# A recurrent layer with its projections inside the head-pair loop, and with them in a phase of their own

## The reference, cut to what matters

```python
def even_layer(h, g, w_in, shift_mu, ...):
    p = rmsnorm(h, g) @ w_in                                   # (1024 x 1024) @ (1024 x 4224)
    p_shift = token_shift(p[..., :SHIFT_WIDTH], shift_mu)      # p + (p_prev - p) * mu
    p_r, p_k, p_v, p_wd, p_ad = jnp.split(p_shift, ...)        # 512, 512, 512, 64, 64 columns
    gate_a, q_b, k_b, v_b, gate_b = jnp.split(p[..., SHIFT_WIDTH:], ...)   # 512 each
    y_a = rwkv7_mix(p_r, p_k, p_v, p_wd, p_ad, ...) * jax.nn.silu(gate_a)
    y_b = chunk_attention(q_b, k_b, v_b, att_bias) * jax.nn.silu(gate_b)
    return h + jnp.concatenate([y_a, y_b], axis=-1) @ w_out

def rwkv7_mix(...):      # 8 heads of 64
    decay = exp(-exp(w(p_wd)));  a = sigmoid(a0 + p_ad @ a2)
    kk = k * k_k, divided by its norm over each head;  k = k * (1 + (a - 1) * k_a)
    state = state * decay + (state @ -kk) (kk * a)^T + v k^T   # a scan over the 1024 tokens
    y = group norm of (state @ r) * lnx_g + lnx_b + bonus(r, k, v)

def chunk_attention(...):  # 8 heads of 64, chunks of 64 tokens, each sees itself and 8 chunks to the left
```

## Time and profile before

| what | us |
|---|---|
| median of 3 runs (4167.7 to 4175.02) | 4168.65 |
| the profiled execution, its own time | 4164.67 |
| its span, first to last instruction | 4162.9 |
| TensorE busy in it | 3959.1 (95%) |
| DVE, ACT, POOL busy | 1739.9, 1324.5, 1197.7 |

### The profile page before, as it was taken

How to read it: one execution, slowest core, us unless ns; L and a number is a source line. 1 busy time by engine, 2 the same in 40 slices (tenths; PEclk the granted TensorE clock), 3 DMA queues, 4 the chain that set the end, 5 groups by cost and what they waited for, 6 DMA issues and landing times.

```text
span 4162.9 us, 59315 instructions
## 1 busy us (share of the span) xinstructions
PE 3959.1 (95%) x26210; PEld 3198.6 (77%) x26210; DVE 1739.9 (42%) x2696; ACT 1324.5 (32%) x2213; POOL 1197.7 (29%) x613
## 2 busy tenths in 40 slices
PE   8899999999999999899999889999999999999997
PEld 4757676665998897677687777897888988888877
DVE  2545454533340258762215463332187432332344
ACT  3232323232332243562212353212275312212133
POOL 1202010102114356761232102343102523332354
PEclk9999999999999999999999999999999999999999
DMA  3101010003111121010011100130100211111111
GB/s 91 32 2 32 2 32 3 17 11 108 42 41 41 51 71 51 26 31 31 28 54 42 40 1 23 49 107 28 51 1 21 72 61 51 47 45 51 51 41 41
DMA packets 164977, 168.68 MB, mean 41 GB/s; under 512 B 8176, under 2 KB 152432, under 8 KB 164720
## 3 DMA queue, kind: packets, MB, share of 16 engines
q1 hardware_dynamic: 164720, 164.89, 12.5%
HBM read 156.48 MB, written 8.39 MB: 40 GB/s over the span
## 4 chain that ended last, share of the span: by engine, by line
PE 80%; DVE 9%; ACT 5%; POOL 4%; issue 2%; DMA 0%; POOLq 0%; DVEq 0%; ACTq 0%; SPq 0%
PE pair L641 16%; PE pair L643 16%; PE pair L642 16%; PE pair L606 10%; PE pair L629 3%; PE pair L617 2%; PE pair L1137 1%; PE pair L596 1%; PE pair L1327 1%; PE pair L791 1%; POOL H L3472 1%; PE pair L1297 1%; ACT BIG L2084 1%; PE pair L783 1%; POOL W_r L3414 1%
## 5 line engine op out<-in xcount | busy, mean ns | idle before, releaser
L641 PE MATMUL pair<-XT_r,W_r 128*128 128x512 f32 x1744 | 693.8, 398 | 8.5 <-ACT BIG L2022 1.9
L642 PE MATMUL pair<-BIG_r,W_r 128*128 128x512 f32 x1624 | 632.2, 389 | 0.0
L3414 POOL TENSOR_TENSOR W_r<-W,W_r 128x2048 fp32r<-128x2048 f32 (+1 forms) x74 | 327.1, 4420 | 741.2 <-ACT W_r L1475 741.2
L643 PE MATMUL pair<-XT_r,W_r 128*128 128x512 f32 x1232 | 480.1, 390 | 0.0
L641 PE MATMUL pair<-W_r,BIG_r 128*128 128x256 f32 (+1 forms) x1280 | 417.9, 326 | 1.5 <-DVE MIX_r L2774 0.4
L606 PE MATMUL pair<-XT,W 128*128 128x512 f32 x928 | 405.5, 595 | 3.2 <-POOL MIX L3287 2.2
L641 PEld LDWEIGHTS pair<-XT_r,W_r 128*128 128x128 f32 x1744 | 327.4, 188 | 85.3 <-issue 10.6
L643 PE MATMUL pair<-W_r,BIG_r 128*128 128x256 f32 (+1 forms) x1152 | 380.3, 330 | 0.0
L642 PEld LDWEIGHTS pair<-BIG_r,W_r 128*128 128x128 f32 x1624 | 305.0, 188 | 68.9 <-issue 6.7
L606 PEld LDWEIGHTS pair<-XT,W 128*128 128x128 f32 x928 | 175.1, 191 | 220.1 <-issue 218.6
L643 PE MATMUL pair<-W_r,MIX_r 128*128 128x256 f32 x960 | 271.6, 283 | 0.0
(11 more groups left out here) (440 smaller groups left out, 7744.3 us busy)
## 6 DMA issues: line engine op xcount, KB each, us to landing
W<-w_in SPq DMA_DIRECT2D x29, 1024.0 KB, 5.5
W<-w_in_e SPq DMA_DIRECT2D x33, 512.0 KB, 6.6
MIX<-w_up SPq DMA_DIRECT2D x15, 1024.0 KB, 5.3
MIX<-w_down SPq DMA_DIRECT2D x15, 1024.0 KB, 4.9
W<-w_in_o SPq DMA_DIRECT2D x12, 1024.0 KB, 5.0
W<-w_in SPq DMA_DIRECT2D x17, 512.0 KB, 4.1
H<-x SPq DMA_DIRECT2D x16, 512.0 KB, 9.2
W<-w_out SPq DMA_DIRECT2D x7, 1024.0 KB, 5.3
```

Of the source, the lines that this page charges most:

```text
L641: E.matmul(b[:, 0:n], lh, rh, start=k == ks[0], stop=False)
L642: E.matmul(b[:, 0:n], lh, rl, start=False, stop=False)
L643: mm = E.matmul(b[:, 0:n], ll, rh, start=False, stop=k == ks[-1])
L3414: G.tensor_tensor(WLO[k % 2][:, 0:n], WSTAGE[k % 2][:, 0:n], WHI[k % 2][:, 0:n], ALU.subtract).then_inc(*s_split.mark("split", k))
```

## The change

It splits the even layer into two phases.

Phase one (`proj`): the normalised rows are kept as a high part `XH` (rounded by ACT) and a low part `XL` (DVE's subtraction). All products of the layer follow one another as split products over 17 weight pieces (`PROJ`): lora, then k, r, v of the recurrence and of the band for two pairs at a time, then both gates. ACT and DVE evict them, gates through Silu, to eight slots in `MIX`; SP writes 29 rows of 128 x 1024 to a tensor `rows` in DRAM. The shifts and the norm of pair 0 run beside.

Phase two: the four head pairs without products. SP loads raw rows, q, k, v and gates back, each behind the operation that frees its buffer. A pair is now "late" (decay, operands, transposes), the factor rounds woven with "tail" (normalising the previous pair; three of its multiplications and additions and the gate go to POOL), and the last chunk rounds woven with "early" (shifts and norm of the next pair). The norm's square root and reciprocal become Ln and Exp on ACT. The pacing is 212 to 192. The keep-up matmuls of the recurrence are removed. `pe_even` keeps only the last tail ahead of the output projection.

```diff
-        RW_ROUNDS, BAND_STEPS = 224, 224
+        RW_ROUNDS, BAND_STEPS = 212, 192
...
-        KEEP_UP.update({("rwkv", "v_tr", c, 0): 14 for c in range(4)})
...
+        PROJ = ([("lora", 0, 0, 1536)] + [(what, g, pp, base + g * HALF + pp * Q) for pp in range(2)
+                                          for what, base in (("rkv", 0), ("qkv", 2176)) for g in (1, 0, 2)] +
+                [(what, 0, pp, base + pp * Q) for what, base in (("gate_r", 1664), ("gate_b", 3712)) for pp in range(2)])
+        FIRST_PIECE = -len(PROJ)
+        SPILL = [(what, g, 2 * pp + ct) for what, g, pp, _ in PROJ[1:] for ct in range(2)
+                 if (what, pp, ct) != ("rkv", 0, 0)]
+        ROW = {b: n for n, b in enumerate(SPILL)}
...
+        def pe_proj():
+            early = pe_early(0)
+            for j, (what, g, pp, _) in enumerate(PROJ):
+                k = FIRST_PIECE + j
+                if (what, g) == ("qkv", 2):
+                    wh, wl = chunk(k)
+                    for t in range(NT):
+                        ts = slice(t * P, (t + 1) * P)
+                        pe_split(proj, every, (what, g, pp, t), Q, KD, lambda kk: (XH[:, kk, ts], XL[:, kk, ts]),
+                                 lambda kk: (wh[:, kk, :], wl[:, kk, :]), done("split", k))
+                else:
+                    width = P if what == "lora" else Q
+                    wh, wl = chunk(k, KD, width)
+                    for c0 in range(0, width, P):
+                        for half in range(2):
+                            hs = slice(half * HALF, (half + 1) * HALF)
+                            pe_split(proj, every, (what, g, 2 * pp + c0 // P, half), HALF, KD,
+                                     lambda kk: (wh[:, kk, c0:c0 + P], wl[:, kk, c0:c0 + P]),
+                                     lambda kk: (XH[:, kk, hs], XL[:, kk, hs]), done("split", k),
+                                     done("ev", "begin", "tr", 4 * half + 3, 1))
+                proj.pe.note("chunk_free", k)
+                if j > 3:
+                    next(early, None)
+            run(early)
...
+        def pe_early(c):
+            ring = for_rw if c else every
+            yield from nothing(3)
+            for hf in range(2):
+                b = ring.open("rwkv", "norm", c, hf)
+                pe.wait_ge(*ring.free("rwkv", "norm", c, hf))
+                pe.wait_ge(*done("rwkv", "kk_sq", c))
+                E.matmul(b[:, :], head_ones[:, :], BT[:, hf * HALF:(hf + 1) * HALF], start=True,
+                         stop=True).then_inc(*rw.pe.mark("rwkv", "norm", c, hf))
+            yield from nothing(3)
...
+        def pe_late(c):
+            for hf in range(2):
+                sl = slice(hf * HALF, (hf + 1) * HALF)
+                for lo, what in ((0, "sig"), (64, "a")):
+                    b = for_rw.open("rwkv", what, c, hf)
+                    pe.wait_ge(*for_rw.free("rwkv", what, c, hf))
+                    pe.wait_ge(*done("rwkv", "lora_ready"))
+                    pe.wait_ge(*done("rwkv", "w_lora2"))
+                    E.matmul(b[:, :], W2[lo:lo + 64, c * P:(c + 1) * P], LT[lo:lo + 64, sl], start=True,
+                             stop=True).then_inc(*rw.pe.mark("rwkv", what, c, hf))
+            yield
+            for hf in range(2):
+                pe_transposes(rw, for_rw, ("v_tr", c, hf), [KTL[:, (hf * 4 + i) * P:(hf * 4 + i + 1) * P]
...
+            for what, src, ready in (("a_tr", RA[:, :, 0, :], "ra"), ("b_tr", tile_pairs(SIG), "ops"),
+                                     ("k_tr", tile_pairs(A), "ops")):
+                if what == "b_tr":
+                    yield
                 for hf in range(2):
+                    pe_transposes(rw, for_rw, (what, c, hf), [src[:, hf * 4 + i, :] for i in range(4)],
+                                  done("rwkv", ready, c))
+            yield
...
+            yield from nothing(8)
+            if c:
+                pe_y_tr(c - 1, R_)
+            yield
+            yield
...
+        def pe_rwkv():
+            after(pe, proj)
+            for c in range(4):
+                yield from pe_late(c)
+                yield from weave(pe_factor(c, 0), pe_tail(c, for_rw))
                 yield from weave(pe_chunks(c, 0), pe_factor(c, 1))
-                yield from pe_chunks(c, 1)
...
+            def high_part(t):
+                for half in range(2):
+                    act.wait_ge(*done("begin", "gained", t, half))
+                    S.activation(XH[:, half * 4:half * 4 + 4, t * P:(t + 1) * P],
+                                 every.bank("begin", "tr", t, half)[:, :].rearrange("p (c n) -> p c n", c=4),
+                                 ACT.Copy).then_inc(*begin.act.mark("begin", "xh", t, half))
...
+        def act_early(c):
+            yield from nothing(2)
+            act.wait_ge(*done("rwkv", "kk", c))
+            if c:
+                act.wait_ge(*done("rwkv", "abt", c - 1, 1, 1))
+            S.activation(BT, KK, ACT.Square).then_inc(*rw.act.mark("rwkv", "kk_sq", c))
+            yield
+            yield
+            for func, scale, by in ((ACT.Ln, NORM_SCALE ** 2, None), (ACT.Exp, -0.5, "unit")):
+                for hf in range(2):
+                    e = BT[:, hf * HALF:(hf + 1) * HALF]
+                    act.wait_ge(*(rw.act.last() if by else done("ev", "rwkv", "norm", c, hf)))
+                    S.activation(e, e, func, scale=scale).then_inc(*rw.act.mark(*("rwkv", by, c, hf) if by else ()))
+            yield
+            yield
...
+        def dve_early(c):
+            yield
+            if c:
+                dve.wait_ge(*done("rwkv", "u0", c - 1, 1))
+            dve_shift(c, 1, K)
+            dve.wait_ge(*rw.dve.last())
+            V.tensor_scalar(KK, K, col("rw_kk", c), None, ALU.mult).then_inc(*rw.dve.mark("rwkv", "kk", c))
+            yield
+            dve_shift(c, 0, R)
+            yield
+            for hf in range(2):
+                dve.wait_ge(*done("rwkv", "norm", c, hf))
+                V.tensor_scalar(BT[:, hf * HALF:(hf + 1) * HALF], (for_rw if c else every).bank("rwkv", "norm", c, hf)[:, :],
+                                1e-24, None, ALU.max).then_inc(*rw.dve.mark("ev", "rwkv", "norm", c, hf))
+            dve_shift(c, 2, KTL)
+            yield
+            yield
+            dve.wait_ge(*done("rwkv", "unit", c, 1))
+            V.scalar_tensor_tensor(KK, KK, NORM_SCALE, BT, ALU.mult, ALU.mult).then_inc(
+                *rw.dve.mark("rwkv", "kk_unit", c))
+            yield
...
+        def dve_late(c):
+            for hf in range(2):
+                hs = slice(hf * HALF, (hf + 1) * HALF)
+                dve.wait_ge(*done("rwkv", "masks"))
+                dve.wait_ge(*done("ev", "rwkv", "sig", c, hf))
+                V.tensor_tensor_scan(CS[:, hs], row_mask, SIG[:, hs], 0.0, ALU.mult, ALU.add).then_inc(
+                    *rw.dve.mark("rwkv", "cs", c))
+            yield
+            dve.wait_ge(*done("ev", "rwkv", "a", c, 1))
+            V.tensor_scalar(T1, A, 1.0, col("rw_ka", c), ALU.subtract, ALU.mult).then_inc(*rw.dve.mark())
+            dve.wait_ge(*rw.dve.last())
+            V.scalar_tensor_tensor(K, T1, 1.0, K, ALU.add, ALU.mult).then_inc(*rw.dve.mark())
+            dve.wait_ge(*rw.dve.last())
...
+            V.tensor_tensor(BT, T1, EX, ALU.mult).then_inc(*rw.dve.mark())
+            dve.wait_ge(*done("rwkv", "v_tr", c, 1))
+            V.tensor_tensor(KTL, K, EX, ALU.mult).then_inc(*rw.dve.mark())
+            wcb = WC.unsqueeze(2).to_broadcast([P, 16, 64])
+            dve.wait_ge(*rw.dve.last())
+            V.tensor_tensor(gn(SIG), gn(BT), wcb, ALU.mult).then_inc(*rw.dve.mark())
+            V.tensor_tensor(gn(A), gn(KTL), wcb, ALU.mult).then_inc(*rw.dve.mark("rwkv", "ops", c))
+            dve_copy_out(rw, for_rw, ("a_tr", c, 1), AN[:, HALF:SEQ], HALF)
...
+        def dve_tail(c, R_):
+            Y = MIX[:, max(c - 1, 0), :]
+            if c:
+                dve.wait_ge(*rw.dve.last())
+                V.tensor_reduce(SM, gn(Y), AX.X, ALU.add).then_inc(*rw.dve.mark())
+                dve.wait_ge(*rw.dve.last())
+                V.tensor_scalar(SM, SM, 1.0 / 64, None, ALU.mult).then_inc(*rw.dve.mark())
+                dve.wait_ge(*rw.dve.last())
+                V.tensor_tensor(gn(Y), gn(Y), SM.unsqueeze(2).to_broadcast([P, 16, 64]), ALU.subtract).then_inc(
+                    *rw.dve.mark("rwkv", "centred", c - 1))
...
+        def pool_proj():
+            pool_split(FIRST_PIECE)
+            pool_masks()
+            pool_split(FIRST_PIECE + 1)
+            after(pool, begin)
+            for raw in RAWB:
+                G.memset(raw[:, 0:1], 0.0).then_inc(*proj.pool.mark("raw_zero"))
+            pool.wait_ge(*proj.pool.last())
+            early = pool_early(0)
+            for j in range(len(PROJ)):
+                if 0 < j < len(PROJ) - 1:
+                    pool_split(FIRST_PIECE + j + 1)
+                if j == 1:
+                    pool.wait_ge(*done("ev", "proj", "lora", 0, 0, 1))
...
```

(44 more changed lines are left out.)

749 lines of the change are left out of this document (360 added, 389 removed).

## The result

The changed kernel takes 4197.78 us (median of 4 runs, 4195.6 to 4199.26) where the kernel before takes 4171.34 beside it: ratio 1.0063, 95% interval 1.0046 to 1.008, so slower by 0.6%. The profiled execution took 4195.6 us, span 4193.3, against 4164.7 for the one of before. The even layer ends at 1049.7 us in place of 1020.9. Of the 30.9 us between the two profiled executions, 28.8 have been lost by then; the remaining three quarters of the kernel take 2.1 us more than they did.

What follows compares the result with a forecast made beforehand. Even layer bound partly by projections, partly by engine-to-engine chains; 401 + 106 + 450 - 14 + 16 + 24 + 10 + 34 = 1027 us against 1021, so about 4175 as a median, range 4138 to 4212.

Steps and rivals of the forecast that it cites:

- forecast case: The prediction's main case for the whole kernel: about 4175 us, own range 4158 to 4192, chance 0.45.
- clock case: Rival: half of factor and chunk time at TensorE's low clock level, costing 40 to 50 us: about 4218; chance 0.20.
- Phase one: All projections as split products: 361.5 us in place of 464, ending at 401, with weights, spills and evictions costing nothing.
- starved phase one: Rival: POOL's masks delay the second weight piece and leave TensorE unfed; chance 0.07 together with late rows.
- Late: Preparation of each head pair without cover, a VectorE chain: 26 us four times plus 2 for first row loads, 106.
- Clock: Each factor stage begins at TensorE's lower clock: two to three us a pair, +10, bounds 0 and 45.
- Tail: Normalising the previous pair within the factor rounds: 5 for each of three pairs, 1 for the first, +16, bounds 3 and 30.
- Band thinner: 192 band steps over 212 rounds: some three steps fewer in a pair's chunk rounds, 1.1 us each, -14, bounds -22 and -8.
- Early: Next pair's shifts and norm in the chunk rounds: 8 us for each of three pairs, +24, bounds 6 and 45.
- End: Fourth pair's tail alone before the output product, POOL first behind the output weights' split: 34 us, bounds 28 and 40.
- slack: Rival, faster: tail and early fall mostly into VectorE's idle time (6 and 12 us), 4136 us; chance 0.28.
- Rows: Rival, slower: each pair's first band step waits for its reloaded rows, +37, 4212; chance 0.07 together with starving.

Runs made afterwards that it cites:

- combined one without filler: Changed kernel plus bonus product in late, tail's POOL work on VectorE (last tail too) and output weights split early, no filler matmuls: 4181.43 us, ratio 1.0024.
- first filler: Changed kernel plus 4, 40 and 14 small filler matmuls per pair in TensorE's waits of the preparation: 4197.0 us, ratio 1.0068 to the kernel before.
- second: The combined one without filler, plus 24 filler matmuls behind the value transposes of each preparation: 4175.23 us, ratio 1.0014 to the kernel before.

## Why the prediction was right, and which terms were not

The forecast was slower, 4175, range 4138 to 4212. The measured 4197.78 lies in the range, and the sign was right. But against its own execution the sum said +6 and the result is +30.9, and 4197.78 lies above the forecast case's own range (4158 to 4192), between it and the clock case. The stated range is 74 us wide and reaches to both sides of no change, and errors of some 36 us one way and 14 the other cancelled in part: that the time lies inside is in part luck. One of the prediction's own signs of being wrong did come, a granted clock under 0.85 in factor rounds (0.77 and 0.82 in the third and fourth pair). Term by term:

- *Phase one*: forecast 37.7 to 401 us, measured 36.2 to 401.3. Right, both the rate of the split products and the cover of weights, spills and evictions. (The terms given for the start, seven times 1.2 and 1, make 9.4 and not 8.7.) The starved phase one did not come.
- *Late*: forecast 26 four times and 2 more, measured 26.3, 25.1, 25.1, 24.5: 101 for 106. Right, VectorE's chain. (The parts named, 19, 4, 2.1 and 2, make 27.1 and not 26.) In the late from 549 ScalarE loads its table for 1.28 us at 550.61 and the sigmoid starts at 551.90. The further 1.38 us of the Trainium skill (ScalarE: Activation LUTs, What ACT_TABLE_LOAD costs), weighed in the prediction, is again not seen.
- *Clock*: forecast +10 with a bound of 45. **This step failed**, by size: it was "Two to three us a pair", for the start of each factor stage only; and the removed keep-up matmuls were put at nothing, where they gave the kernel before some 11 us. The runs price the clock without any edit. The kernel before ran 23 times beside the first experiments, from 4158.3 us at a mean clock of 0.985 to 4176.34 at 0.981, and a line through all 23 has 2.96 us per 0.001 (19 runs beside the second group: 2.95). 0.001 of the mean over some 4170 us is 8.3 us on the lower level, so each such us costs 0.36. The factor and chunk rounds spend 89 us more there than before (146 for 57): 32 us. The price fits two pairs of stages with the same instructions at two clocks. The second pair's rest took 87.1 us at 0.86 and, in the run with two of late's operations on POOL, 81.9 at 0.94:

```profile
622.00:704.00 82.00, 70.54 (x1077) 59.09 (x1072) 52.82 (x122) 34.65 (x76) 16.23 (x18) 0.94 0.03 7
```

That is 5.2 us for 14.6 less at the lower level, 0.36 of it; the fourth pair's rest without and with filler gives 5.4 for 17.4, 0.31. By these the clock's share is 28 to 32 us. It is worked out, and no run took all of it away; other kernels of the experiments give less per 0.001 over their own spread (0.9 us with the tail cut, 2.0 in the combined one without filler). Where filler raised the clock it gave back 8.5 us in the rounds (first filler) and 6 in the whole (second).
- *Tail*: forecast 16. **The second step that failed**: "5 for each of three pairs, 1 for the first", from VectorE's, POOL's and the Sqrt's work. Taking 0.36 us off for each us at the lower level, the factor rounds are 35.1, 39.8, 37.7 and 38.3 us, for 30.1 before in the first pair and 30.2 in the others: 5.0, 9.6, 7.5 and 8.1, together 30. What was left out is TensorE's part. The bonus product stands in the same chain (1.95 us of TensorE in the row below); moving it took 3.5 us off the first pair's rounds, 2.2 by this reckoning.

```profile
578.50 1.95 PE L763 MATMUL pair<-head_ones,XT 128*128 128x2 f32 x16 [0.85 <-DVE W L2782]
```

With the elementwise work cut away the rounds of pairs 2 to 4 were still 7.3, 9.4 and 5.2 us over those of before, or 6.0, 6.5 and 3.7 by this reckoning, so that work is worth 9 of the 30 us. Eight transposes of the tail and their copies stand there too; no run separates them.
- *Band thinner*: forecast -14. In the fourth pair, which has no early, the rest takes 73.8 us by the same reckoning (83.5 less 9.7) for 77.2 before: -3.4, four times -14. Right, but hidden by the clock (0.84 for 0.92). At 0.91, in the experiments with the tail on VectorE and with it cut, the same rounds took 77.5 us in full.
- *Early*: forecast 24. The rest of the other three pairs is 78.2, 78.3 and 81.0 by this reckoning, for 77.5, 77.4 and 77.3: with the 3.4 of the band added back, 4.1, 4.3 and 7.1, together 16. Over-sized; cutting early gave 16 to 18 with the clock that came back.
- *End*: forecast 34, measured 32.8, in the order forecast: POOL behind the split of the weights.

So the sum of 1027 was off by +22 (clock), +14 (tail), -8 (early), -5 (late) and -1 (end): 1049, where the product starts at 1049.7. How much of the clock's share is itself due to tail and early, in whose waits it sinks, is not separated: with the tail cut the factor rounds' clock went from 0.77 to 0.88 up to 0.90 to 0.95.

Of the rivals, slack did not absorb it. "The clock stays low" was half right: its condition (over a quarter of the rounds at the low level) held, 146 of 515 us, and its price of 40 to 50 us, reckoned for half of the time, came out at 28 to 32. It was taken as an alternative to the forecast, with a chance of 0.20, where it was an addition to it. The Trainium skill (TensorE: Matmul & The Clock Gate, HAM oscillation) charges half of the throttled time, 45 us for the 89; the runs show 0.31 to 0.36 of that time. Rows did not come late: the one wait on a load, 6.2 us in the first late, stood in a stage of 26.3, 1.2 longer than the next.

## What to carry to other kernels

When dense work is taken out of the gaps of a serial chain, the gaps become exposed and TensorE's clock sinks in them; count the time at the lower level before and after, and take its price from the spread of identical runs. List what is moved by engine, TensorE included: a product of 16 columns that sat under a full TensorE becomes a link when it is moved into a chain. Filler for the clock pays only at a place where nothing behind it in TensorE's order is about to become ready, and spreading secondary work evenly can be worth more than finishing it early (17 us here).
